# First mixer of a hybrid decoder: dilation-1 attention in natural blocks, both heads of a pair per item, statistics merged once per pair

## The reference

```
for g, (window, dilation) in enumerate(((128, 1), (512, 4), (2048, 16))):
    # keys gathered by stride `dilation`, banded causal window of 128 sub-steps plus self
    logits = q @ k.T * 64 ** -0.5 + rel_table[rel_bucket(distance)]
    logits = where(valid, logits, -inf)
    lse_g = logsumexp(logits);  out_g = exp(logits - lse_g) @ v
alpha = softmax(stack(lse), axis=0)          # over the three groups
o = sum_g alpha_g * out_g                    # then o @ w_o, residual
```

## Time and profile before

| | |
|---|---|
| median of 3 runs | 1847.71 us |
| profiled execution, span | 1841.6 us |
| outside the span | 6.1 us |
| TensorE matmul busy | 97% of the span, 8593 instructions |
| VectorE, ScalarE, GpSimd busy | 52%, 34%, 4% |
| steps 1 to 8 of the first mixer | 81.8 to about 745 us |

### The profile page before, as it was taken

How to read it: one execution, slowest core, us unless ns; L and a number is a source line. 1 busy time by engine, 2 the same in 40 slices (tenths; PEclk the granted TensorE clock), 3 DMA queues, 4 the chain that set the end, 5 groups by cost and what they waited for, 6 DMA issues and landing times.

```text
span 1841.6 us, 23032 instructions
## 1 busy us (share of the span) xinstructions
PE 1784.8 (97%) x8593; PEld 1452.0 (79%) x8593; DVE 959.9 (52%) x1577; ACT 630.9 (34%) x951; POOL 69.2 (4%) x58
## 2 busy tenths in 40 slices
PE   7998999999999997899999999999998999999997
PEld 5886878878888876688888888788886888888886
DVE  6443444444444433754454556677777635454554
ACT  5232323333233322422222244456655212222343
POOL 2000000000000000200000011000002000000011
PEclk9998999999999998999999999999999999999998
DMA  5664222222222322233333333323222333333332
GB/s 142 187 154 112 71 82 77 77 71 70 82 67 74 91 82 82 69 95 93 99 95 98 93 107 98 103 81 91 80 60 69 101 93 102 92 102 91 102 100 73
DMA packets 313706, 170.66 MB, mean 93 GB/s; under 512 B 5812, under 2 KB 308461, under 8 KB 313581
## 3 DMA queue, kind: packets, MB, share of 16 engines
q1 hardware_dynamic: 295102, 157.13, 29.9%
q10 hardware_dynamic: 18528, 12.45, 2.3%
HBM read 167.27 MB, written 15.92 MB: 99 GB/s over the span
## 4 chain that ended last, share of the span: by engine, by line
PE 83%; DMA 11%; DVE 4%; ACT 1%; SPq 0%; issue 0%; POOL 0%; ACTq 0%
PE unit_out L1158 22%; PE unit_out L1160 22%; PE unit_out L1159 22%; DMA bias_tiles_a<-bias_vectors 5%; DMA w_raw<-in_a_w_o_dram 4%; PE attn L1316 4%; PE turned L1234 3%; PE logits L1158 2%; DMA bias_tiles_b<-bias_vectors 1%; DVE act_lo L855 1%; PE logits L1269 1%; PE logits L1160 1%; PE logits L1159 1%; PE attn L1437 1%; DMA w_raw<-in_a_w_qkv_dram 1%; PE misc L1234 1%
## 5 line engine op out<-in xcount | busy, mean ns | idle before, releaser
L1158 PE MATMUL unit_out<-act_hi,w_hi 128*128 128x512 f32 x2024 | 808.1, 399 | 12.3 <-DVE act_lo L855 10.3
L1160 PE MATMUL unit_out<-act_hi,w_lo 128*128 128x512 f32 x2024 | 790.8, 391 | 0.0
L1159 PE MATMUL unit_out<-act_lo,w_hi 128*128 128x512 f32 x2024 | 790.4, 391 | 0.0
L1158 PEld LDWEIGHTS unit_out<-act_hi,w_hi 128*128 128x128 f32 x2024 | 382.5, 189 | 102.0 <-DVE act_lo L855 13.4
L1160 PEld LDWEIGHTS unit_out<-act_hi,w_lo 128*128 128x128 f32 x2024 | 381.4, 188 | 81.3
L1159 PEld LDWEIGHTS unit_out<-act_lo,w_hi 128*128 128x128 f32 x2024 | 382.2, 189 | 77.3 <-issue 2.4
L617 ACT ACTIVATE w_hi<-w_raw 128x1024 fp32r<-128x1024 f32 (+3 forms) x259 | 273.9, 1057 | 478.6 <-PE unit_out L1160 345.5
L840 DVE TENSOR_TENSOR w_lo<-w_raw,w_hi 128x1024 fp32r<-128x1024 f32 (+3 forms) x259 | 323.8, 1250 | 137.7 <-ACT w_hi L617 137.4
L602 POOL TENSOR_TENSOR sumsq<-sumsq,square 128x512 f32<-128x512 f32 x49 | 68.3, 1394 | 1761.3 <-ACT square L635 1759.6
L1316 PE MATMUL attn<-probs_t,heads 128*64 128x128 f32 x768 | 102.9, 286 | 21.6 <-ACT probs_t L661 21.5
L731 ACT ACTIVATE act_hi<-hidden 128x512 fp32r<-128x512 f32 x64 | 40.5, 633 | 243.2 <-DVE hidden L1003 243.2
(11 more groups left out here) (169 smaller groups left out, 1250.5 us busy)
## 6 DMA issues: line engine op xcount, KB each, us to landing
w_raw<-in_w_ff_dram SPq DMA_DIRECT2D x128, 512.0 KB, 4.0
w_raw<-in_a_w_qkv_dram SPq DMA_DIRECT2D x72, 512.0 KB, 3.8
w_raw<-in_b_w_qkv_dram SPq DMA_DIRECT2D x24, 512.0 KB, 3.7
bias_tiles_a<-bias_vectors SPq DMA_DIRECT2D x16, 576.0 KB
w_raw<-in_w_ple_gate_dram SPq DMA_DIRECT2D x16, 512.0 KB, 4.0
bias<-bias_tiles_a ACTq DMA_DIRECT2D x14, 576.0 KB, 4.3
bias_tiles_b<-bias_vectors SPq DMA_DIRECT2D x8, 512.0 KB
bias<-bias_tiles_b ACTq DMA_DIRECT2D x8, 512.0 KB, 3.6
```

The source lines that it names most:

```text
L1158: te.matmul(bank, w_k[0], hi, start=start, stop=False)
L1159: te.matmul(bank, w_k[0], lo, start=False, stop=False)
L1160: return te.matmul(bank, w_k[1], hi, start=False, stop=stop)
```

## The change

Dilation-1 attention leaves the residue order. Its Q, K and V are now stored in natural order (blocks of 128 positions), by a permuted access pattern in the evacuation. The items become four **phases** for a pair, each over both heads j:

- phases 0 and 1 (near): dilation 1, two query blocks each; a block takes its own and the previous block's keys (256; 128 for block 0).
- phases 2 and 3 (far): dilations 4 and 16, two residue tiles each.

Score phases 0 to 3 stand in slots 0 to 3. Transposes and values stand in slots 5 to 8 in the order 2, 3, 0, 1, eight each (six in phase 0). All four phases have a `probs` buffer of their own; `v_t`, `gain_rows`, `table` and `lam_in` move into other buffers to make room.

A query's near row and far row lie on different partitions, so the minima and sums are merged once per pair in slot 4: VectorE spreads the near statistics (slot 3), four matmuls with a 128x32 matrix `fold` bring them to residue order (`far_ps`), VectorE and ScalarE form the joint minimum, the factors and the reciprocal, and after the unit four more such matmuls (`near_ps`) bring the near factors back. Probabilities are multiplied by their factor one slot before their transposes.

The bias vector is shorter (four matmuls' worth of columns instead of six). Expansion is per pair on the SyncE queue: for each head four DMAs of 32 KB and one of 128 KB. Loading a pair's bias is five DMAs, now on the SyncE queue too. The second mixer's bias loads move from ScalarE's to SyncE's queue, with a wait for the scores that last used the buffer. SyncE's loops are unrolled.

```diff
-A_ITEMS = 2 * NT
+A_ITEMS = NT
+A_SCORES = range(A_ITEMS)
+A_MERGE = A_ITEMS
+A_VALUES = {5: 2, 6: 3, 7: 0, 8: 1}
...
+            def expand_a(pair):
+                sp.wait_ge(vectors_ready, 16)
+                for h in (2 * pair, 2 * pair + 1):
+                    for r in range(NT):
+                        sp.dma_start(
+                            tiles_a.ap()[h, r * SUB:(r + 1) * SUB, 0, :].rearrange("l (r c) -> r l c", r=NT),
+                            bass.AP(vectors, h * VEC + (NT - 1 - r) * NEAR + SUB - 1,
+                                    [[NEAR, NT], [-1, SUB], [1, 2 * SUB]])).then_inc(tiles_ready, 16)
+                    sp.dma_start(tiles_a.ap()[h, :, 1, :].rearrange("p (g c) -> g p c", g=2),
+                                 bass.AP(vectors, h * VEC + RHOS * NEAR + P - 1,
+                                         [[BLK, 2], [-1, P], [1, P]])).then_inc(tiles_ready, 16)
...
+            for u in range(2, A_PAIRS * A_UNITS):
                 load_a(At(u // A_UNITS), At(u), u % A_UNITS)
...
+                if u == 5:
+                    expand_a(0)
+                if u == 7 or u > A_UNITS and u % A_UNITS == 3:
+                    load_bias_a(u // A_UNITS)
+                if u == 8 or u > A_UNITS and u % A_UNITS == 6 and u // A_UNITS < A_PAIRS - 1:
+                    expand_a(u // A_UNITS + 1)
...
+                    if i == 0:
+                        sp.wait_ge(logits_done, ITEMS_A + max(head - 1, 0) * B_ITEMS)
+                        sp.dma_start(bias[head % 2][:, :].rearrange("p (j c) -> p j c", c=T),
...
+            def scores_a(par, ph):
+                q, k = a_parts(1 - par, Q), a_parts(1 - par, K)
+                for h in range(2):
+                    tile = 2 * (ph % 2) + h
+                    mine = slice(tile * P, (tile + 1) * P)
+                    if ph < 2:
+                        keys = slice(max(tile - 1, 0) * P, (tile + 1) * P)
+                        end = (h + 1) * BLK
+                        first = end - (keys.stop - keys.start)
+                        for n, (a, b) in enumerate(((0, 0), (0, 1), (1, 0))):
+                            for j in range(2):
+                                rows = slice(j * E, (j + 1) * E)
+                                last = te.matmul(logits[:, j * T + first:j * T + end], q[a][rows, mine],
+                                                 k[b][rows, keys], start=n == 0, stop=n == 2)
+                    else:
+                        for g in range(1, GROUPS):
...
+            def values_a(par, ph):
+                for h, c, j, col in a_tiles(ph):
...
+                    last = te.matmul(to, a_buf(1 - par, g, V)[:, keys * P + j * E:keys * P + (j + 1) * E],
+                                     by, start=ph == 2 and h == 0 and c == 0,
+                                     stop=ph == 1 and h == 1 and c == 1)
...
+                if has_attn and i in A_SCORES:
                     if i == 0:
                         wait(te, qk_ready, s.times(2))
-                        wait(te, v_ready, s.times(GROUPS))
...
+                    if i == 2:
+                        wait(te, evac_done, s.times(A_UNITS))
+                    wait(te, logits_done, t)
+                    scores_a(par, i).then_inc(scores_ready, 1)
+                if has_attn and i == A_MERGE:
...
+                    wait(te, v_ready, s.times(GROUPS) if not has_proj else (s + 1).times(GROUPS))
+                    wait(te, spread_stat_ready, s)
+                    for b in range(NT):
+                        last = te.matmul(
+                            misc[b * SUB:(b + 1) * SUB, 0:4 * NT].rearrange("p (a r) -> p a r", r=NT),
+                            fold[:, :],
...
+                if has_attn and i in A_VALUES:
+                    ph = A_VALUES[i]
+                    wait(te, probs_ready, (s - 1).times(A_ITEMS) + (i - 4))
+                    turn(turned, [(col, probs[ph][:, col:col + P]) for _, _, _, col in a_tiles(ph)]
+                         ).then_inc(turned_ready, 1)
```

More of the change, by code:

```diff
@@ L25 @@
+import itertools
 import math
@@ L111, in bias_selector @@
 def bias_selector():
+    near = 2 * SUB - 1 - np.arange(NEAR)
     off = P - 1 - np.arange(BLK)
     dists, valid = [], []
-    for delta in range(NT - 1, -NT, -1):
-        d = NT * off + delta
+    for rho in range(NT - 1, -NT, -1):
+        d = NT * near + rho
         dists.append(d)
@@ L248, in build @@
         hidden = sb("hidden", [P, T])
-        v_t = [sb(f"v_t{i}", [P, T]) for i in range(2)]
         ident = sb("ident", [P, P])
@@ new lines, in load_bias_a @@
+            def load_bias_a(pair):
+                par = pair % 2
+                sp.wait_ge(tiles_ready, (pair + 1) * TILE_LOADS * 16)
+                wait(sp, logits_done, (pair - 1) * A_ITEMS)
+                halves = bias[par][:, :].rearrange("p (j x c) -> p j x c", j=2, x=2)
+                for j in range(2):
+                    for b in range(2):
+                        sp.dma_start(
+                            halves[:, j, 0, b * P:(b + 1) * P].rearrange("p (r l) -> p r l", r=NT),
+                            tiles_a.ap()[2 * pair + j, :, 0, :].rearrange(
+                                "p (r b l) -> p b r l", r=NT, b=2)[:, b, :, :]).then_inc(bias_ready[par], 16)
+                sp.dma_start(halves[:, :, 1, :], tiles_a.ap()[2 * pair:2 * pair + 2, :, 1, :].rearrange(
+                    "j p c -> p j c")).then_inc(bias_ready[par], 16)
@@ L1070, in sub_b @@
                         head = s - 1 if par else s - 2
-                        wait(ve, bias_ready[1 - par], (head.half() + (A_PAIRS + 1)).times(16))
+                        wait(ve, bias_ready[1 - par], (head.half() + (A_PAIRS // 2 * BIAS_LOADS + 1)).times(16))
                     wait_apart(ve, scores_ready, t + 1, (s_small, 16 * SMALL))
@@ L1258, in sub_a @@
                             te.wait_ge(ple_ready, 2)
-                    else:
-                        wait(te, logits_done, t)
-                    tile = slice(r * P, (r + 1) * P)
-                    (q_hi, q_lo), (k_hi, k_lo) = a_parts(1 - par, Q), a_parts(1 - par, K)
-                    passes(logits[:, 0:T], (q_hi[rows, tile], q_lo[rows, tile]), k_hi[rows, :],
-                           k_lo[rows, :], True, True)
-                    for g in range(1, GROUPS):
-                        if i == 0:
-                            wait(te, evac_done, s.times(A_UNITS) - 2 * (GROUPS - 1 - g))
-                        last = te.matmul(logits[:, T + (g - 1) * P:T + g * P],
-                                         a_buf(1 - par, g, Q)[rows, tile],
-                                         a_buf(1 - par, g, K)[rows, tile], start=True, stop=True)
@@ L1272, in sub_a @@
-                    last.then_inc(scores_ready, 1)
-                if has_attn and i > 0:
-                    wait(te, probs_ready, t)
-                    turn(turned, [(c * P, probs[(i - 1) % 2][:, c * P:(c + 1) * P])
-                                  for c in range(NT + 2)]).then_inc(turned_ready, 1)
+                    if i == 2:
+                        wait(te, evac_done, s.times(A_UNITS))
+                    wait(te, logits_done, t)
+                    scores_a(par, i).then_inc(scores_ready, 1)
```

338 lines of the change are left out of this document (219 added, 119 removed).

## The result

Four runs of the changed kernel took 1724.46 to 1726.6 us, median 1725.07; four of the kernel before, on the same chip, 1842.35 to 1848.53, median 1846.49. The ratio is 0.9354 [0.9338, 0.9369]. In the two profiled executions the span went from 1841.6 to 1723.1 us: 118.5 less, where the sum had 94.8. In every run with both figures, device time is 1.8 us above the span; of the 6.1 us called "outside the span" in the table of the kernel before, the other 4.3 are that its profiled execution was faster than the median.

What follows compares the result with a forecast made beforehand. TensorE, busy in 97% of the span, was taken as the bound. Gains of 71 (five middle steps), 15.3 (steps 0 and 1) and 11.5 (end), less 3 for stalls, made 94.8; from the median 1847.7 that gave 1753 us, range 1738 to 1798.

Steps and rivals of the forecast that it cites:

- The queue: SyncE's weight loads behind a pair's ten expansion DMAs: 17 us per pair, losing 9 us at the start, 3 in six steps.
- Rival 5: SyncE's queue: no stall by the expansions at all, start included but for 3 us; time 1744, chance 0.10.
- The terms of the step: A middle step of the first mixer, priced part by part on TensorE: 66.0 us in place of 80.2, gain 14.2.
- values: Value matmuls of a step, 48 become 30, neighbours on different column halves partly overlapping: 4.4 us, between 3.7 and 7.3.
- the merge: Eight small matmuls per step that join near and far statistics: 1.0 us in all, bounds 0.4 and 1.7.
- Far scores: 16 fp32 matmuls per step, now 8 pairs on the two row halves: 2.4 us, or 4.3 if pairs don't overlap.
- near scores: Dilation-1 scores, 24 passes of 512 columns become 18 of 256 and 6 of 128: 1.8 us, between 1.5 and 2.9.
- the V wait: Slot 4, ahead of the small matmuls: TensorE stands still 0.9 us for ScalarE's copy of the third V tile.
- The start: Before the first scores: four bias-vector matmuls for six gain 1.8 us; late weight loads were charged 9.
- Step 8: Output projection's loads wait behind eight expansions at 12.65 us each, which set the pace: no gain.
- Second mixer: Bias loads now hold SyncE until the previous head's last scores are reduced: no cost, at worst 8 us.
- Rival 3: Expansion DMAs: a 256 B run costs two of 512 B, 7.2 us more per pair; time 1789, chance 0.10.

## Why the prediction was right or wrong

*What bounds the kernel*: right. TensorE's work was the time in every step, and the gain came where TensorE has less to do.

*The queue*: this step failed, and it is half of the 23.7 us by which the sum fell short. "If depth in runs counts and landings don't overlap, a pair takes 23 us; if bytes count, 12.65. I take 17" became 9 us lost at the start and 3 in the steps. None of the 12 occurred: from 33 us to the first scores TensorE had no idle time, and in a step none behind unit 6. The two rows it went by the earlier trace rows both show DMAs that wait for the one before; the new ones don't wait, which was in the diff. Ten issues took 8.1 us, the load behind them landed at 15 and not at 20, and a stall begins at 22, where the forecast had 23. At the start the two expansions (41.79 to 49.9 in the queue, and from 59.52) hid in the same way, with units of only 5.6 us around them. Rival 5 said so with a chance of 0.10; it deserved more than the middle of the range did.

*The terms of the step*: 66.0 against 64.58, 1.4 too much, over all 9.4 us (7 of it in steps 2 to 6, 1.4 in step 1, 1.0 up to the first expansion for the second mixer). Two terms carry it: values 4.4 against 3.9, because matmuls on the two column halves run side by side almost wholly (1.02 us for eight is 128 ns each, about half of 243) and not as the nearest row did; the merge 1.0 against 0.4, because a small matmul with 32 weight columns takes 28 ns a record, where the nearest row, with 128 weight columns, had 101. That the weight columns make the difference is likely and not shown. Far scores were 2.2 against 2.4, near scores 1.8 as forecast, transposes 3.2 as forecast (0.85 for eight), the V wait 0.8 against 0.9. The 80.2 that stands for a middle step of the kernel before was a little too high: step 2 still had 2.4 us of the clock and the stall of step 1 in it.

*The start*: 4.2 us earlier where 1.8 were forecast, of which 1.4 were the missing matmuls; the rest goes with the granted clock.

*Step 8*: no gain, as forecast, and the loss of 1.7 there and the gain of 1.5 behind it cancel. *Second mixer*: nothing, as forecast.

In the spans: 12 (queue) + 9.4 (steps) + 2.4 (start) - 0.2 (step 8 and behind it) is 23.6 of 23.7. The rest between 1753 and 1725 is that a gain in spans was taken from a median: the span before lay 6.1 us below the median used, the one after 2.0.

The range was too narrow below. Its lower end, 1738, was some 6 us under rival 5 alone, while the step's terms had lower bounds of their own (values 3.7, merge 0.4, near scores 1.5) and they leaned the same way. Rival 5 at 1744 with those three at their lower bounds, 1.6 us in seven steps, is 1733; without the 3 us that rival 5 still kept for the start it is 1730. The start's clock (2.4) and the offset between span and median (4.1) lead to 1723.5, and a measurement's own spread should have been in the range too. Rival 3 was priced with 7.2 us more per pair, for which no working stands.

## What to carry to other kernels

DMAs that don't wait for each other cost the queue their issue (here 0.6 to 1.9 us each, ten in 8.1) and not their landing; price a burst by how late the next load behind it lands, against when a stall begins, and not by the spacing of transfers that wait. Look at the outermost dimension of a DRAM to DRAM copy before its bytes: two against sixteen was worth 43.7 us here, more than a third of what the whole change brought. And when several terms of a sum are set by the nearest rows and all have room on one side, put the low end of the range where they all take it.

## What the runs showed of the hardware

- Full-height fp32 matmuls that write the two halves of the columns overlap as neighbours (eight in 1.02 us, 243 ns each alone). Sorted by half, four in a row on each side, eight take 1.51, because the second half's matmuls start 0.49 us after the first's, when two of the first four are still to come: still less than the 1.94 of no overlap. The same with the halves of the rows: 1.09 and 1.64.
- A DRAM to DRAM copy of 32 KB in four blocks takes 2.3 us from issue to the next when it is waited for, 128 KB in two blocks 4.8, 512 KB in two blocks 13.0, 512 KB in sixteen blocks lands 4.6 us after its issue. Over 4.5 us with one of two blocks alone under way, 0.14 of the 16 DMA engines was busy.
- TensorE's granted clock was 0.84 over a stretch in which it waited for a transfer in each slot, and 1.00 over the same work without the waits. After single standstills of 3.3, 6.5, 11.4 and 13.8 us TensorE ran at the lower level for a while, and the stall's price was 1.6 to 3.6 us above the standstill. Between 20 and 35.5 us of nine traces with the same code up to there the granted clock was 0.74 to 1.00 with no cause that these runs show.
